# Low part of every weight slot moved from GpSimd to VectorE in a two-model, four-layer float32 kernel

## What is computed

```python
# first_block
for layer in range(DEPTH):
    u = rms_norm(h, norm_mix_pre[layer])
    m = shortconv_fox_mixer(u, ...) if layer % 2 == 0 else conformer_conv_module(u, ...)
    h = h + rms_norm(m, norm_mix_post[layer])
    f = swiglu_ffn(rms_norm(h, norm_ffn_pre[layer]), ...)
    h = h + rms_norm(f, norm_ffn_post[layer])
# second_block
h = h + hgrn2_mixer(rms_norm_2(h, hg_norm), ...);            h = h + conv_ffn(rms_norm_2(h, ffn_norm[0]), ...)
k, v = shared_kv(h, kv_norm, w_kv)
h = h + swa_sink_attention(rms_norm_2(h, attn_norm), k, v, ...); h = h + conv_ffn(rms_norm_2(h, ffn_norm[1]), ...)
return rms_norm_2(h, final_norm)
```

## Time and profile before

| | |
|---|---|
| Median of three runs | 2476.34 us |
| The profiled execution's own time | 2479.11 us |
| Its span, first to last instruction | 2477.3 us |
| TensorE busy | 2385.5 us (96%) |
| VectorE busy | 1284.6 us (52%) |
| GpSimd busy | 1000.5 us (40%), 935.9 us of it in 376 low parts |
| ScalarE busy | 834.4 us (34%) |

### The profile page before, as it was taken

One profiled execution on the slowest core, in us unless ns is written; L12 is line 12 of the kernel. 1 busy time (PEld: TensorE's weight loads), 2 busy tenths in 40 slices (PEclk: granted clock), 3 DMA queues, 4 the chain that ended last, 5 costly groups with the idle time before them and its releaser, 6 DMA issues.

```text
span 2477.3 us, 30996 instructions
## 1 busy us (share of the span) xinstructions
PE 2385.5 (96%) x11218; PEld 1914.2 (77%) x11218; DVE 1284.6 (52%) x1612; ACT 834.4 (34%) x1222; POOL 1000.5 (40%) x416
## 2 busy tenths in 40 slices
PE   8999999999898899999999999999999879999997
PEld 6777788888564688888778887888888767888886
DVE  6563644401534554441166585677721796677701
ACT  6443322222323332222242254333222564333322
POOL 3224444444542544444443222444544223444543
PEclk9999899999898999999989999999999999999999
DMA  4212233333263223333222111333333212333332
GB/s 153 61 60 85 72 97 93 101 94 94 79 164 85 68 94 93 97 98 94 89 76 78 52 52 54 97 95 95 100 93 94 71 35 68 100 95 94 101 94 76
DMA packets 68001, 216.12 MB, mean 87 GB/s; under 512 B 11600, under 2 KB 12112, under 8 KB 67920
## 3 DMA queue, kind: packets, MB, share of 16 engines
q1 hardware_dynamic: 67632, 214.63, 28.9%
q10 hardware_dynamic: 288, 0.36, 0.0%
HBM read 210.64 MB, written 4.33 MB: 87 GB/s over the span
## 4 chain that ended last, share of the span: by engine, by line
PE 90%; DVE 7%; ACT 2%; issue 1%; DMA 0%; DVEq 0%; SPq 0%
PE bank L458 27%; PE bank L460 27%; PE bank L459 27%; PE bank L723 2%; PE bank L816 2%; DVE h L1423 1%; DVE ds L1933 1%; DVE u_lo L1405 1%; ACT ds L1339 1%; DVE small L1914 1%; DVE dq L1883 0%; DVE m L1413 0%; PE bank L656 0%; DVE acat_lo L1392 0%; PE bank L849 0%
## 5 line engine op out<-in xcount | busy, mean ns | idle before, releaser
L398 POOL TENSOR_TENSOR w_lo<-raw,w_hi 128x1024 fp32r<-128x1024 f32 x376 | 935.9, 2495 | 1431.5 <-ACT w_hi L976 1431.2
L458 PE MATMUL bank<-u_hi,w_hi 128*128 128x512 f32 x1952 | 773.5, 396 | 19.5 <-DVE u_lo L1405 18.3
L459 PE MATMUL bank<-u_lo,w_hi 128*128 128x512 f32 x1952 | 766.3, 393 | 0.0
L460 PE MATMUL bank<-u_hi,w_lo 128*128 128x512 f32 x1952 | 765.9, 392 | 0.0
L976 ACT ACTIVATE w_hi<-raw 128x1024 fp32r<-128x1024 f32 x378 | 395.4, 1056 | 991.9 <-PE bank L460 912.1
L458 PEld LDWEIGHTS bank<-u_hi,w_hi 128*128 128x128 f32 x1952 | 370.6, 190 | 107.0 <-DVE u_lo L1405 23.6
L460 PEld LDWEIGHTS bank<-u_hi,w_lo 128*128 128x128 f32 x1952 | 370.3, 190 | 78.3
L459 PEld LDWEIGHTS bank<-u_lo,w_hi 128*128 128x128 f32 x1952 | 370.8, 190 | 76.9 <-issue 1.2
L458 PE MATMUL bank<-hid_hi,w_hi 128*128 (+1 forms) x704 | 278.1, 395 | 0.0
L460 PE MATMUL bank<-hid_hi,w_lo 128*128 (+1 forms) x704 | 278.1, 395 | 0.0
L459 PE MATMUL bank<-hid_lo,w_hi 128*128 (+1 forms) x704 | 278.1, 395 | 0.0
(11 more groups left out here) (270 smaller groups left out, 2464.2 us busy)
## 6 DMA issues: line engine op xcount, KB each, us to landing
raw<-weights_dram SPq DMA_DIRECT2D x378, 512.0 KB, 3.5
bz<-gated_dram SPq DMA_DIRECT2D x32, 270.0 KB, 4.5
gated_dram<-bz SPq DMA_DIRECT2D x8, 272.0 KB, 2.1
h<-x_t_dram SPq DMA_DIRECT2D x8, 256.0 KB, 6.1
out_dram<-m SPq DMA_DIRECT2D x8, 256.0 KB, 2.2
ap<-select_dram SPq DMA_DIRECT2D x1, 512.0 KB, 8.3
vec<-vectors_dram SPq DMA_DIRECT2D x1, 343.0 KB, 7.3
cmask<-masks_dram ACTq DMA_DIRECT2D x1, 224.0 KB, 2.4
```

What stands on the lines that cost most here:

```text
L398: pool.tensor_tensor(w_lo[:, j, :], raw[:, j, :], w_hi[:, j, :].bitcast(F32), ALU.subtract)\
L458: pe.matmul(out, wh, xh, start=start, stop=False)
L459: pe.matmul(out, wh, xl, start=False, stop=False)
L460: return pe.matmul(out, wl, xh, start=False, stop=stop)
```

## The change

GpSimd forms no low part of a weight any more; it keeps the post-norms, the clearing of `bwv`, the blocks of taps and three pieces of the output. VectorE forms all 378. At the head of a pre-normed stage it forms the low parts of places 3 to 5 (`first_lows`) ahead of its wait for the root; elsewhere `low_over(s)` forms that of slot s+3 at a place that is written into its order, and in a post-norm head the one of place 2 stands behind `norm_add`. The diff, cut to its core (the stages of q and k, `b_in`, `c_fq`, `c_i`, `c_g` and the residual additions get `low_over` lines in the same manner):

```diff
@@ -393,20 +393,6 @@
         @block.gpsimd
         def _(pool):
-            def low_part(s, j):
-                pool.wait_ge(hi_ready, s + 1)
-                pool.tensor_tensor(w_lo[:, j, :], raw[:, j, :], w_hi[:, j, :].bitcast(F32), ALU.subtract)\
-                    .then_inc(w_ready, 1)
-            def low_parts(a, b):
-                if b - a >= RING:
-                    with pool.Fori(0, (b - a) // RING) as i:
-                        for n in range(RING):
-                            low_part(RING * i + a + n, (a + n) % RING)
-                for s in range(b - (b - a) % RING, b):
-                    low_part(s, s % RING)
             def norm_output(stat):
                 pool.wait_ge(rs_ready, RS[stat] + 1)
@@ -423,28 +409,14 @@
                 cols = eye[:, :].unsqueeze(1).to_broadcast([P, GROUPS * STEPS, 32])
                 pool.tensor_tensor(bw[:, b, :, :], rows, cols, ALU.mult).then_inc(bw_ready, 1)
-            pool.wait_ge(w_ready, DVE_SLOTS)
-            low_parts(DVE_SLOTS, SLOT["a_ffn_in"] + AHEAD - 1)
             norm_output("a_post")
-            low_parts(SLOT["a_ffn_in"] + AHEAD - 1, SLOT["b_in"] + AHEAD - 1)
             norm_output("a_fpost")
-            low_parts(SLOT["b_in"] + AHEAD - 1, SLOT["b_in"] + AHEAD)
             pool.memset(bwv[:, :, :], 0.0).then_inc(taps_zeroed, 1)
-            for n in range(2 * KC):
-                s = SLOT["b_in"] + AHEAD + n
-                low_part(s, s % RING)
-                if n == 1:
-                    pool.wait_ge(taps_landed, 16 * SHIFTS * (GROUPS + 1))
-                if 1 <= n <= CONV_RING:
-                    tap_blocks(n - 1)
-                if n % 2 and n // 2 >= CONV_RING:
-                    tap_blocks(n // 2)
-            low_parts(SLOT["b_out"] + AHEAD, SLOT["b_ffn_in"] + AHEAD - 1)
+            pool.wait_ge(taps_landed, 16 * SHIFTS * (GROUPS + 1))
+            for c in range(KC):
+                tap_blocks(c)
             norm_output("b_post")
-            low_parts(SLOT["b_ffn_in"] + AHEAD - 1, SLOT["c_fq"] + AHEAD - 1)
             norm_output("b_fpost")
-            low_parts(SLOT["c_fq"] + AHEAD - 1, N_SLOTS)
             pool.wait_ge(rs_ready, RS["final"] + 1)
             for c in POOL_LAST:
...
@@ -1380,6 +1352,22 @@
         @block.vector
         def _(dve):
+            def low_part(s, i=0):
+
+                j = s % RING
+                dve.wait_ge(hi_ready, s + RING * i + 1)
+                dve.tensor_tensor(w_lo[:, j, :], raw[:, j, :], w_hi[:, j, :].bitcast(F32), ALU.subtract).then_inc(w_ready, 1)
+
+            def low_over(s, i=0):
+
+                if s + AHEAD < N_SLOTS:
+                    low_part(s + AHEAD, i)
+
+            def first_lows(s):
+
+                for n in range(3):
+                    low_over(s + n)
+
             def split_value(name, c, make):
...
@@ -1443,6 +1431,8 @@
                 for n in range(KC):
                     dve.wait_ge(slot_done, SLOT[part] + n + 1)
                     keep_chunk(stat, n, bank[n % 4], bias(n) if bias else None)
+                    if n < KC - 1:
+                        low_over(SLOT[part] + n)
             def add_out(l):
...
@@ -1468,6 +1461,7 @@
                     if split:
                         scaled_low(split, 4 * half + 3)
                         sum_squares(stat, range(max(4 * half, 1), 4 * half + 4))
+                    last_back(l, half)
             def feed_forward(l, second):
...
@@ -1496,6 +1490,8 @@
                                 dve.wait_ge(gconv_ready, CONVG[l] + 2 * j + 1)
                             dve.scalar_tensor_tensor(out=gconv[:, b, back:], in0=ut[:, b, 0:T - back], scalar=w,
                                                      in1=gconv[:, b, back:], op0=ALU.mult, op1=ALU.add).then_inc(gconv_ready, 1)
+                    if not isinstance(i, int):
+                        low_over(s0 + 2 * b, i)
                     dve.wait_ge(slot_done, s0 + 2 * j + 2)
                     dve.wait_ge(gate_ready, HID[l] + j + 1)
                     dve.tensor_tensor(ut[:, b, :], gconv[:, b, :], bank[2 * b + 1][:, :], ALU.mult).then_inc(ht_ready, 1)
@@ -1506,16 +1502,35 @@
                     dve.tensor_scalar(hi, ut[:, b, :], 1.0, None, ALU.mult).then_inc(hh_ready, 1)
                     dve.wait_ge(hh_ready, HID[l] + j + 1)
                     dve.tensor_tensor(lo, ut[:, b, :], hi.bitcast(F32), ALU.subtract).then_inc(hid_ready, 1)
+                    if not isinstance(i, int) or b:
+                        low_over(s0 + 2 * b + 1, i)
+
+                first_lows(s0)
                 pair(0, 0)
                 pair(0, 1)
                 with dve.Fori(1, FC // 2) as i:
                     for b in range(2):
                         pair(i, b)
+            def way_back(l, half):
+
+                s = SLOT[f"{l}_ffn_out"] + HALF * half
+                with dve.Fori(0, 2) as i:
+                    for n in range(RING):
+                        low_over(s + n, i)
+                for n in range(2 * RING, HALF - 1):
+                    low_over(s + n)
+
+            def last_back(l, half):
+                low_over(SLOT[f"{l}_ffn_out"] + HALF * (half + 1) - 1)
+
             def keep_ffn(l, stat):
-                for n in range(KC):
-                    keep_chunk(stat, n, ffn_full(dve, l, n))
+                for half in range(2):
+                    way_back(l, half)
+                    for n in range(4 * half, 4 * half + 4):
+                        keep_chunk(stat, n, ffn_full(dve, l, n))
+                    if not half:
+                        last_back(l, half)
             dve.memset(ones[:, :], 1.0).then_inc(consts_made, 1)
...
@@ -1525,13 +1540,15 @@
             for c in range(KC):
                 if c < DVE_SLOTS:
-                    dve.wait_ge(hi_ready, c + 1)
-                    dve.tensor_tensor(w_lo[:, c, :], raw[:, c, :], w_hi[:, c, :].bitcast(F32), ALU.subtract).then_inc(w_ready, 1)
+                    low_part(c)
                 scaled_low("a_pre", c)
+            for c in range(DVE_SLOTS, AHEAD):
+                low_part(c)
             sum_squares("a_pre")
             dve.wait_ge(wf_ready, 1)
             dve.tensor_tensor(wf_lo[:, :, :, :], wf, wf_hi[:, :, :, :].bitcast(F32), ALU.subtract).then_inc(wf_ready, 1)
+            first_lows(0)
             dve.wait_ge(rs_ready, RS["a_pre"] + 1)
...
@@ -1619,6 +1641,7 @@
                         dve.wait_ge(sconv, 4 * c + 4)
                         split_value("a_gate", c, lambda dst: dve.tensor_tensor(dst, ay[:, :], bank[2][:, :], ALU.mult))
                         low_of("a_gate", c, acat_lo[:, c, :], acat_hi[:, c, :])
+                    low_over(SLOT["a_conv"] + n)
                 own, c = rows_of(hd % 2), 4 + hd // 2
                 hi, lo = (x[own, c, :].rearrange("p (b n) -> p b n", n=P) for x in (acat_hi, acat_lo))
                 found = bank[3][:, :].rearrange("p (b n) -> p b n", n=P)
@@ -1627,13 +1650,16 @@
                     dve.tensor_tensor(l_, src[r], h_.bitcast(F32), ALU.subtract).then_inc(ol_ready, 1)
             keep_out("a_out", "a_post")
             norm_add("a_mix", "mix_post", 0, "a_fpre", "a_fpre")
+            low_over(SLOT["a_ffn_in"] - 1)
             feed_forward("a", None)
             keep_ffn("a", "a_fpost")
             norm_add("a_ffn", "ffn_post", 0, "b_pre", "b_pre")
+            low_over(SLOT["b_in"] - 1)
 
             dve.memset(bz[:, :, 0:LONG_TAPS - 1], 0.0)
             dve.memset(bz[:, :, LONG_TAPS - 1 + T:], 0.0)
+            first_lows(SLOT["b_in"])
             dve.wait_ge(rs_ready, RS["b_pre"] + 1)
...
@@ -1848,8 +1888,10 @@
             add_ffn("c", "d_pre", "d_kv")
 
+            low_over(SLOT["d_kv"])
             for c in range(KC):
                 scaled_low("d_q", c)
+            low_over(SLOT["d_kv"] + 1)
             for e in range(2):
                 none = ones[rows_of(1 - e), 0:1].unsqueeze(2).to_broadcast([64, 2, T])
...
@@ -1887,6 +1929,8 @@
             query_evac(1)
             query_low(0)
             query_low(1)
+            low_over(SLOT["d_q"])
+            low_over(SLOT["d_q"] + 1)
             dve.wait_ge(dist_landed, 16)
             def pairs_of(x):
@@ -1945,6 +1989,7 @@
                     window_add(c + 1)
                 window_probs(c)
                 if c + 2 < KC:
+                    low_over(SLOT["d_q"] + c + 2)
                     query_low(c + 2)
                 if c + 1 < KC:
                     window_max(c + 1)
```

22 lines of the change are left out of this document (added).

## The result

| | before | after |
|---|---|---|
| median of the runs on one chip | 2479.12 us (8 runs, 2475.97 to 2480.39) | 2485.7 us (8 runs, 2481.25 to 2486.69) |
| profiled execution, span | 2479.11, 2477.3 us | 2483.57, 2481.4 us |

The ratio is 1.0026 with a 95% interval of 1.0015 to 1.0037: slower by 6.6 us, where I had forecast +1.2 us. The forecast time was 2477.5 us, worked out from the median of three runs before, 2476.34 us; with eight runs that median is 2479.12 us, so 2.8 of the 8.2 us between forecast and result are not the change's. The spans of the profiled executions lie 4.1 us apart. GpSimd is now busy for 63.2 us. VectorE is busy for 1343.9 us, only 59 us more than before, though its 376 new low parts take some 460 us: its other operations have become some 400 us shorter, nearly all of it where TensorE does not wait for them.

What follows compares the result with a forecast made beforehand. TensorE was taken as the bound, busy 2385.5 of 2477.3 us. Terms -6.8 - 2.1 - 0.8 + 2.2 + 8.7 = +1.2 us on the median 2476.34 gave 2477.5 us, range 2467.5 to 2485.5.

Steps and rivals of the forecast that it cites:

- Three post-norm heads: +2.2 us: At `a_ffn_in`, `b_ffn_in`, `c_fq`: third slot's low part, behind the sums, makes TensorE 0.7 to 0.8 us late each.
- A gain of a half microsecond from TensorE's second piece is swallowed by this wait.: At the three post-norm heads: time gained at TensorE's second piece vanishes in its wait for the third slot's low part.
- Rival 2: Clock falls at the three other post-norm heads after a longer TensorE wait: 7.5 us more, 2485 us; chance 0.10.
- my own gap: At the three post-norm heads: a forecast TensorE gap of 1.2 us, under the 2 us at which the clock held.
- The head of `b_in`: +8.7 us: At `b_in`: GpSimd's taps take turns with VectorE's sums, third slot +6.1 us, then low clock 2.5 us.
- Layer d: -6.8 us: Layer d's window attention: rounds fall from 12.82 to 11.9 us (-3.3), about -3.5 us in all ahead of them.
- Layer a's attention: -2.1: Layer a: three TensorE waits for probabilities, 1.23 us each, shorten by 0.6 to 0.7 us as `acat_lo` runs unblocked.
- Sums behind ffn_out: -0.8: Behind `a_ffn_out` and `b_ffn_out`: two TensorE waits for sums of squares end some 0.4 us earlier.
- 0.28, 0.45 and 0.27: Whole kernel: chances of faster (below 2471.4 us), within about 0.2% of no change, and slower (above 2481.3 us).
- rival 4: Blockings worth more than counted, for instance in layer d's first rounds or layer c: 2470 us; chance 0.07.

Runs made afterwards that it cites:

- experiment 1: Changed kernel, with the third slot's low part formed ahead of the sums of squares at the four post-norm heads: 2465.12 us, ratio 0.9948.
- Experiment 2: Changed kernel, with GpSimd's first blocks of taps formed only after the sixth low part of `b_in`'s slots: 2479.54 us.
- experiment 8: Changed kernel, with the low parts of six weight slots in layer d's window rounds back on GpSimd: 2490.64 us.
- experiment 3: Changed kernel with the edits of experiment 1 and Experiment 2 together: 2458.53 us, ratio 0.9928.
- experiment 9: On experiment 3, in layer d's window rounds the next slot's low part formed behind the next round's row maxima: 2452.58 us.
- experiment 10: On experiment 3, VectorE forms all eight of the post-norm's products with the root, in place of two: 2451.48 us.
- experiment 11: On experiment 3, VectorE forms five of the post-norm's eight products with the root, GpSimd three: 2448.25 us.
- experiment 12: The best version: changed kernel with the edits of experiment 1, Experiment 2, experiment 9 and experiment 11 together: 2444.48 us, ratio 0.9864.
- experiment 4: experiment 1's kernel with three unread VectorE products ahead of the fourth residual sum at the four post-norm heads, putting a TensorE gap back: 2467.84 us.
- experiment 5: experiment 4's kernel with one unread product of 64 columns more, widening TensorE's gap: 2469.52 us.
- experiment 6: Kernel before the change, with GpSimd's third low part at the four post-norm heads waiting until the norm's input is split: 2479.47 us.
- experiment 7: Changed kernel, with low parts of slots four to six of the eight pre-normed stages formed behind the root wait: 2512.54 us, ratio 1.0152.

## Why the prediction was wrong

**The step that failed is "Three post-norm heads: +2.2 us": the low clock behind TensorE's wait was put at nothing.** The first half of the step held: the third slot's low part is ready when I said (the first of the three in the row above ends at 266.8 us, 29.2 us behind the post-norm's mean square, where I had 269.1 - 239.8 = 29.3), and the third slots begin 0.9, 0.6 and 0.7 us later than before, 2.2 us in all. The error lies in the sentence "A gain of a half microsecond from TensorE's second piece is swallowed by this wait." I saw that TensorE's gap of a half microsecond would go and counted it as time, not as something that acts on the clock. Without it the rise comes 3.1 to 5.5 us after TensorE's start instead of 8.7 to 9.5, TensorE is through its first two slots earlier, and so its wait for the third slot's low part was 2.8 to 3.8 us, not 0.7 to 0.8. Behind such a wait the clock fell, which I had excluded for a gap of 1.2 us, and the third slots took 2.7, 1.8 and 2.6 us longer. Measured: 2.2 + 7.0 = 9.2 us for 2.2. That VectorE's order, with the low part behind the sums, makes the wait is shown by experiment 1.

Rival 2 named just this ("because TensorE comes up to speed sooner and stands 3 us") with 0.10 and priced it at 7.5 us, for 7.0 measured. That its 2485 is also where the time came out is partly luck: the median before was 2.8 us higher than the one that it started from, and 2.9 us of gains that nobody forecast, below, went the other way. The argument against it used my own gap, which rested on the clock of before.

**The head of `b_in`: +8.7 us** was right in place, cause and size: 7.8 us, of which 5.7 (I had 6.1) are the third slot's later start and 2.1 (I had 2.5) the low clock. The blocks of taps ran in one piece of 6.99 us from 649.07; this head begins 1.1 us later than before, so that is 648.0 on the prediction's axis, where I had 647.8. (The prediction's 645.9 for the last transfer is a slip: 649.04 less 2.7 is 646.3.) Two sums took 2.27 us each, the low part 2.98, and the clock was at half until 661.4. That the wait was 8.4 and not 6.7 us is the failed step again: TensorE was through its first two slots sooner. Experiment 2 shows the taps' part in the loss, 5.2 us. The early low part alone takes the head to 33.7 us too, as it is then formed before the blocks begin, but there the low clock behind the wait of 2.4 us falls into the next stretch, which takes 192.9 us in place of 188.7.

**Layer d: -6.8 us**, measured -7.1: -3.4 ahead of the first normalization (I had -3.5) and -3.8 in the rounds (I had -3.3). The rounds went to 11.84 for 11.9, and experiment 8 shows their cause. The Trainium skill, in "GPSIMD Engine Reference", section "Key points", has VectorE and GpSimd share their SBUF interfaces, with contention for VectorE's instructions that have two SBUF inputs or run in a 2-port perf mode. The trace agrees that they block each other, with 4.16 us for 2.06; the normalizations that are blocked have one tensor input, so they are not the case of two inputs, and no trace names an instruction's mode. **Layer a's attention: -2.1**, measured -2.0, the waits 0.6 us in place of 1.23. **Sums behind ffn_out: -0.8**, measured -0.3 for each of two. Of the chances, 0.28, 0.45 and 0.27, the first two should read 0.27 and 0.46 by their own terms.

**Not predicted: -2.1 us in the rest of layer b's mixer.** Behind the layernorm's waits the clock is low for a while, and where no low clock from the head reaches into this stretch the profiled executions fall into two groups: it took 188.7 to 189.4 us in the changed kernel and in experiments 2, 3, 9, 10, 11 and 12, and 190.8 and 190.9 before and in experiment 8, with the same waits of TensorE. The clock was low for 6.8 us of it in the changed kernel and for 13.7 us before. (Experiments 1, 4, 5, 6 and 7 took 191.3 to 195.6 us, with a low clock or a wait at its start.) What puts a kernel into one group was not tried. It hid part of the loss in the profiled execution. Layer c's mixer took 0.8 us less, 0.5 of it a wait for `ca` that is gone; rival 4 had named layer c.

One part of the change stood in no term of the prediction: without forming the three low parts ahead of the root the change would have cost 27 us more (experiment 7).

## What to carry to other kernels

When a change removes a short gap on TensorE in a stretch where its clock is low, work out the arrival at the next hand-over again with the clock rising earlier: all that was just in time may be late, and a wait of 2.4 us and more there costs half of the following 3 to 6 us as well. On an engine that several wait for, the operation that TensorE wants first goes ahead of sums that nobody wants yet: moving one low part of 1.2 us ahead of five microseconds of sums was worth 20 us over four heads. And where GpSimd's operations run beside VectorE's operations on data in SBUF, count GpSimd's work as VectorE's; taking more of it back (here three of the six products with the root) gained another 10 us, though not all of it should go: with all six it was 7 us.

## What the hardware showed unexpectedly

- While TensorE's granted clock was 0.50, a gap of 0.50 us and more put the rise off by some 4 us in seven of seven heads (in an eighth the clock rose inside the gap), one of 0.45 us in none of four. At full clock, gaps of 0.55 us in every 2.2 us left it at 1.00.
- The clock was at half behind gaps of 2.4 to 8.4 us, and behind the single gap of 1.3 us at each head of experiment 10 it had not fallen. In experiments 11 and 12, with three gaps of 1.0 to 1.5 us close together, it fell at seven heads of eight, so the longest gap alone doesn't tell.
- One normalization of 0.35 us on VectorE took 2.45 us beside a subtraction of 2.41 us on GpSimd.
- Over the whole span the mean granted clock is 0.983 after, 0.989 in the best version and 0.995 with all eight products on VectorE, which is not the fastest: a high clock alone isn't time.
